# Gate products in halves around the update product of a triangular inverse, and five of ten conditioning quarters summed on GpSimd

## The reference, cut to what matters

```python
c_act = jax.nn.silu(c)
for layer in range(DEPTH):
    ada = c_act @ ada_w[layer] + ada_b[layer]             # 1024 x 6144 weights
    sh1, sc1, gt1, sh2, sc2, gt2 = jnp.split(ada, 6, axis=-1)
    h = modulate(rmsnorm(x, norm_mix_w[layer]), sh1, sc1)
    x = x + gt1[:, None, :] * token_mixer(h, ...)
    ...
# in token_mixer
t_mat = lax.linalg.triangular_solve(eye + lmat, eye, left_side=True, lower=True, unit_diagonal=True)
...
y = jax.nn.sigmoid(g_a) * (o_a @ w_a_out) + jax.nn.sigmoid(g_b) * (o_b @ w_b_out)
```

## Time and profile before

| | |
|---|---|
| median of 3 runs | 1731.92 us (1731.67 to 1734.11) |
| profiled execution | 1731.27 us, its span in the trace 1729.4 us |
| mean granted clock of PE | 0.989 |
| busy in the span: PE, DVE, ACT, POOL | 96%, 85%, 63%, 4% |
| the inverse of layer 0 in the trace | 134.14 to 199.09 us |
| the inverse of layer 1 | 609.24 to 674.18 us |
| the experts | from about 757 us to the end |

### The profile page before, as it was taken

How to read it: one execution, slowest core, us unless ns; L and a number is a source line. 1 busy time by engine, 2 the same in 40 slices (tenths; PEclk the granted TensorE clock), 3 DMA queues, 4 the chain that set the end, 5 groups by cost and what they waited for, 6 DMA issues and landing times.

```text
span 1729.4 us, 26895 instructions
## 1 busy us (share of the span) xinstructions
PE 1663.6 (96%) x10359; PEld 1447.7 (84%) x10362; DVE 1471.6 (85%) x1475; ACT 1084.4 (63%) x947; POOL 74.7 (4%) x132
## 2 busy tenths in 40 slices
PE   6998899999999988999999999999999999999997
PEld 6977799999998778987788888888888888888875
DVE  6979688887858696879998998999899989989998
ACT  4565345433445653566677777777777777777775
POOL 5010000000000100000000010000000000100000
PEclk8999999999999999999999999999999999999999
DMA  9746566888845365679999999999999999999994
GB/s 310 249 152 200 169 238 229 304 280 287 290 148 169 100 204 172 210 261 354 342 379 378 365 392 374 365 398 367 373 394 366 373 391 360 385 392 355 394 394 164
DMA packets 261449, 519.99 MB, mean 301 GB/s; under 512 B 12170, under 2 KB 75892, under 8 KB 261364
## 3 DMA queue, kind: packets, MB, share of 16 engines
q1 hardware_dynamic: 257988, 506.21, 82.2%
q0 software_dynamic: 3376, 12.58, 1.8%
HBM read 510.90 MB, written 7.86 MB: 300 GB/s over the span
## 4 chain that ended last, share of the span: by engine, by line
PE 80%; DVE 15%; issue 2%; ACT 2%; DMA 1%; POOL 0%; SPq 0%; DVEq 0%; ACTq 0%; POOLq 0%
PE bank L1156 17%; PE bank L1158 17%; PE bank L1157 17%; PE bank L1162 7%; PE bank L1163 7%; PE bank L1164 7%; DVE w_lo L1855 3%; DVE ada_acc L1873 3%; DVE w_lo L2048 2%; PE bank L1782 1%; DMA ring<-in_ada_w_dram 1%; ACT w_hi L1078 1%; PE bank L1312 0%; DVE hT_lo L1975 0%; DVE smax L2126 0%
## 5 line engine op out<-in xcount | busy, mean ns | idle before, releaser
L2048 DVE TENSOR_TENSOR w_lo<-ring,w_hi 128x2048 fp32r<-128x2048 f32 x336 | 764.3, 2289 | 84.0 <-ACT w_hi L1078 82.4
L1078 ACT CAST w_hi<-ring 128x2048 fp32r<-128x2048 f32 x336 | 643.3, 1915 | 125.0 <-PE bank L1158 113.5
L1156 PE MATMUL bank<-w_hi,xg_hi 128*128 128x512 f32 x896 | 353.0, 394 | 1.9 <-DVE w_lo L2048 1.0
L1158 PE MATMUL bank<-w_hi,xg_lo 128*128 128x512 f32 x896 | 349.2, 390 | 0.0
L1157 PE MATMUL bank<-w_lo,xg_hi 128*128 128x512 f32 x896 | 348.8, 389 | 0.0
L1162 PE MATMUL bank<-hT_hi,w_hi 128*128 128x256 f32 x1040 | 298.0, 287 | 8.1 <-DVE w_lo L1855 7.4
L1163 PE MATMUL bank<-hT_lo,w_hi 128*128 128x256 f32 x1040 | 292.2, 281 | 0.0
L1164 PE MATMUL bank<-hT_hi,w_lo 128*128 128x256 f32 x1040 | 292.0, 281 | 0.0
L1855 DVE TENSOR_TENSOR w_lo<-ring,w_hi 128x2048 fp32r<-128x2048 f32 x94 | 214.1, 2288 | 34.5 <-ACT w_hi L787 34.2
L787 ACT CAST w_hi<-ring 128x2048 fp32r<-128x2048 f32 x94 | 179.2, 1909 | 60.5 <-PE bank L1164 57.1
L1162 PEld LDWEIGHTS bank<-hT_hi,w_hi 128*128 128x128 f32 x1040 | 198.0, 190 | 12.4 <-issue 6.1
(11 more groups left out here) (451 smaller groups left out, 1903.5 us busy)
## 6 DMA issues: line engine op xcount, KB each, us to landing
ring<-in_moe_w_gate_dram SPq DMA_DIRECT2D x112, 1024.0 KB, 7.3
ring<-in_moe_w_up_dram SPq DMA_DIRECT2D x112, 1024.0 KB, 7.4
ring<-in_moe_w_down_dram SPq DMA_DIRECT2D x112, 1024.0 KB, 7.2
ring<-in_ada_w_dram SPq DMA_DIRECT2D x48, 1024.0 KB, 5.8
ring<-in_w_in_dram SPq DMA_DIRECT2D x38, 1024.0 KB, 5.8
ring<-in_ffn_w_gate_dram SPq DMA_DIRECT2D x14, 1024.0 KB, 5.7
ring<-in_ffn_w_up_dram SPq DMA_DIRECT2D x14, 1024.0 KB, 5.9
ring<-in_ffn_w_down_dram SPq DMA_DIRECT2D x14, 1024.0 KB, 5.4
```

What stands on the lines that cost most here:

```text
L1078: act.copy(w_hi[MOE_BUF[p % NS_MOE]][:], ring[:, p % RING, :]).then_inc(hi_ready, 1)
L1156: pe.matmul(o, xh, wh, start=start, stop=False)
L1158: return pe.matmul(o, xl, wh, start=False, stop=stop)
L2048: dve.tensor_tensor(w_lo[b][:], ring[:, p % RING, :], f32(w_hi[b][:]), ALU.subtract).then_inc(taken, 1)
```

## The change

It has four parts.

1. In the inverse, `two_blocks` of the gate unit becomes one block ahead of the update product and one behind it. The gate units' banks alternate for it (`GATE_BANK`), and each first half waits for an earlier sigmoid.
2. POOL sums five quarters: 5, 7 and 9 of layer 0, 4 and 10 of layer 1. For each unit it multiplies the four pieces in place in the ring, adds the upper half to the lower (128x1024) and the two pieces that are left (128x512) into `pool_acc`; for kh = 1 there is one more 128x512 addition. DVE still folds these quarters (`fold_from_pool`), each together with the next quarter of its own, except quarter 9. POOL begins with the transposed L of the inverse (`l0_ps`), and begins a further quarter when its last one is folded. SP waits for POOL's sum where it reloads such a slot.
3. Unit kh = 1 of quarter 9 moves from behind the first two mix units to between wb0 and wb1.
4. At the end of the dense SwiGLU, `ada_sum` moves one iteration ahead on PE, and DVE's `adac`, scale and router weights move from behind the loop into its last iteration.

```diff
+    GATE_BANK = (0, 0, 2, 0, 2, 0, 1)
...
+            if l == 0 and cc == 0:
+                ada_units(l, 1)
...
-                if l == 0 and (kh, cc) == (0, 1):
-                    ada_units(l, 1)
...
+    pool_q = ((5, 7, 9), (4, 10))
...
+            def sum_units(l):
+
+                for n, q in enumerate(pool_q[l]):
+                    if n == 0:
+                        pool.wait_ge(l0_ps, l + 1)
+                    else:
+                        pool.wait_ge(ada_folded, part_of[(l, pool_q[l][n - 1])] + 1)
+                    for kh in range(2):
...
+                        for kk in range(4):
+                            ins = pool.tensor_scalar(w[:, kk, :], w[:, kk, :], c_silu[:, 4 * kh + kk:4 * kh + kk + 1],
+                                                     None, ALU.mult)
+                        link(ins)
+                        link(pool.tensor_tensor(w[:, 0:2, :], w[:, 0:2, :], w[:, 2:4, :], ALU.add))
+                        if kh == 0:
+                            ins = pool.tensor_tensor(pool_acc, w[:, 0, :], w[:, 1, :], ALU.add)
+                        else:
+                            link(pool.tensor_tensor(w[:, 0, :], w[:, 0, :], w[:, 1, :], ALU.add))
+                            ins = pool.tensor_tensor(pool_acc, pool_acc, w[:, 0, :], ALU.add)
+                        ins.then_inc(pool_sum, 1)
...
-                    pe.wait_ge(gate_s, 8 * l + lev)
-                    two_blocks(("gate", l, lev), 0)
+                    pe.wait_ge(gate_s, 8 * l + max(lev - 1, 1))
+                    one_block(("gate", l, lev), GATE_BANK[lev], 0)
...
+                    one_block(("gate", l, lev), GATE_BANK[lev], 1)
-                pe.wait_ge(xx_s, 11 * (l + 1))
+                pe.wait_ge(xx_s, 12 * (l + 1))
...
-                        if i == 2 * FC - 1:
+                        if i == 2 * FC - 2:
                             ada_sum(8, 16, 3, 2 * P + 2)
...
+                if key in by_pool:
+                    return
...
+                    if ("ada", l, q - 1, 1) in by_pool and (l, q) != (0, NQ - 2):
+                        fold_from_pool(l, q - 1)
...
                 ahead(("wa", l, 1), 0)
+                if l == 0:
+                    fold_from_pool(0, 9)
...
                         ahead(("fg", i), 2)
+                        if i == 2 * FC - 1:
+                            ada_groups(1, 3, 2 * P + 2, (FFN_Q[:4], FFN_Q[4:]), NQA + 3)
+                            dve.wait_ge(ada_s, 4)
+                            norm_scale(2)
+                            fold_router()
```

More of the change, by code:

```diff
@@ L1 @@
+import itertools
 import math
@@ L117, in build_program @@
     u_of = {k: n for n, (k, _) in enumerate(units)}
+    pool_q = ((5, 7, 9), (4, 10))
+    by_pool = {("ada", l, q, kh) for l in range(L) for q in pool_q[l] for kh in range(2)}
+    took = list(itertools.accumulate(k not in by_pool for k, _ in units))
+    summed = list(itertools.accumulate(k in by_pool for k, _ in units))
+    T0 = took[-1]
     part_of = {}
@@ L292, in build_program @@
         XT_s = wk(9216, TB * H // 2, P)
+        pool_acc = wk(10240, 512)
         X = wk(8192, TB * H, P)
@@ L580, in load @@
                 if u >= RING:
-                    sp.wait_ge(taken, u - RING + 1)
                     old = units[u - RING][0]
+                    if old in by_pool:
+                        sp.wait_ge(pool_sum, summed[u - RING])
+                    else:
+                        sp.wait_ge(taken, took[u - RING])
                     if old[0] == "ada" and old[1] == 0 and old[2] < NQA - 1:
@@ L1878, in take, with fold, fold_from_pool @@
                 if kh == 1 and n >= NQA:
[L1879 to L1886 removed]
+                    if ("ada", l, q - 1, 1) in by_pool and (l, q) != (0, NQ - 2):
+                        fold_from_pool(l, q - 1)
+                    dve.wait_ge(taken, took[u])
+                    fold(part_of[(l, q)], acc)
+            def fold(m, acc):
+                if m:
+                    dve.wait_ge(ada_folded, m)
+                link(dve.transpose(ada_acc[:, 1, :], acc))
+                dve.tensor_reduce(ada_part[:, 16 * m:16 * m + 16],
+                                  ada_acc[:, 1, :].rearrange("p (b i) -> p b i", i=32), AX.X,
+                                  ALU.add).then_inc(ada_folded, 1)
+            def fold_from_pool(l, q):
+                dve.wait_ge(pool_sum, summed[u_of[("ada", l, q, 1)]])
+                fold(part_of[(l, q)], pool_acc)
             def take_upto(u):
```

42 lines of the change are left out of this document (19 added, 23 removed).

## The result

The changed kernel takes 1743.89 us (median of 3 runs, 1743.46 to 1747.07) against 1731.92 before: a ratio of 1.0072, 95% interval 1.0059 to 1.0086. The forecast was 1731.4 with a range of 1721 to 1738: the time is 12.5 us above the forecast and outside the range. The profiled execution took 1743.46 us at a span of 1741.7.

A forecast was written before the change was run, and what follows sets the result against it. DVE was taken to bound levels 1, 2, 3 and 5 of the inverse, PE the rest. Layer 0 +2.5, layer 1 -0.4 and SwiGLU's end -2.6 gave -0.5: 1730.8 profiled, 1731.4 as median, range 1721 to 1738.

The forecast's parts named there:

- 128x512 would take 0.58; I take 0.6: Price of POOL's one-input multiply, scaled from casts at 0.77 ns an element; its price may lie between 0.45 and 1.3.
- The dear rival: POOL's multiply takes 0.9 us or more, deciding from about 0.75; quarters 2.4 longer, total 1738; chance 0.22.
- the hold on level 4's scaling: Inverse level 4: DVE's path 7.9, about 9.0 with holds of 0.3 and 0.6; PE needs 9.1, so -0.8.
- Branches and fold, layer 0: Layer 0: branches +2.4 from POOL's holds, fold of quarter 9 +3.3, mix -1.2.
- The term of +3.3: Fold of quarter 9: DVE waits 2.4 for POOL and folds 1.4; PE's mix starts 3.3 later, bounds 0 and 6.
- Recurrence, layer 0: Recurrence of layer 0: DVE's path makes it 16.3 instead of 17.2, so -0.9.
- rival *clock: Waits of 3 us at the mix and 2.7 behind level 6 bring the low clock, 1 to 1.7 each: 1735; chance 0.08.
- Who stops whom: DVE instructions with two SBUF operands and POOL's wait for each other to the end; those with a PSUM operand are free.
- level 6: Level 6 to the recurrence's first product: 13.6 against 12.9, +0.7; a wait for ACT replaces one for DVE.
- Level 3: Inverse level 3: fold of quarter 5 adds 1.4, split held 0.5, scaling 0.6; +2.4, giving 12.5.
- The start of level 1: Start of the inverse's level 1: POOL's addition holds DVE, so U starts 0.9 later; bounds 0 and 1.3.
- The SwiGLU's end: End of the dense SwiGLU: the fold moves into DVE's idle time, last squares end sooner; -2.6 (-2 to -3.2).

The follow-up runs named there:

- copy kernel: Changed kernel with POOL's 40 multiplies by a column replaced by copies; total not compared, mixers 7.4 and 0.3 us longer than in the kernel before.
- POOL at one column: Changed kernel with POOL's multiplies and additions cut to one column of each tile; total not compared, mixers gain 2.5 and 1.1 us against the kernel before.
- late-fold kernel: Changed kernel with DVE's fold of quarter 9 moved ahead of the last mix unit's split: 1741.69 us, 1.0046 of the kernel before.
- the token copies first: Changed kernel with ACT's four token copies ahead of the sigmoid of gate unit 6: 1737.61 us, 1.0029 of the kernel before.
- the halves with the token copies first: Changed kernel without POOL's quarters, unit 9.1 back at the mix, ACT's token copies ahead of gate unit 6's sigmoid: 1724.28 us, 0.9948 of the kernel before.

## Why the prediction was wrong

**The mis-sized term: POOL's multiply.** The step that failed is "For one input ... 128x512 would take 0.58; I take 0.6". The casts were the wrong nearest row: the lone price is 1.56 us, above even the upper bound of 1.3 from the two-input rows. The prices for two inputs held (1.2 and 2.2 put in; 1.26 alone, 2.35 to 2.4 in after). The dear rival had the mechanism, from 0.75 us on, but its 0.9 us gave 1738; at the same 6.6 us for each 0.3, the upper bound of 1.3 that the prediction itself named would give an estimated 1747, and the range ended at 1738. The copy kernel shows what hung on it: 8.6 us. The Trainium skill, GPSIMD Engine Reference, section Engine selection, calls one-input forms "roughly line-rate". The copy, 610 ns, is 1.4 times the 0.43 us estimated from that, and the multiply by a column or a constant, 1564 and 1487 ns, 3.6 and 3.5 times: the measurement decides, and the page does not hold for this form.

**The second mis-sized term: the hold on level 4's scaling.** The sum had DVE's path in level 4 "with holds of 0.3 and 0.6 about 9.0", and the level at 9.1. It took 10.97 and 10.98 us in after, and 11.38 and 11.37 in the copy kernel, where POOL had the price of the sum: 2 us in either layer. DVE's split, scaling and update in layer 0 of after, POOL's addition beside them, and the stretch of level 4 in layer 1:

```profile
171.53 2.29 DVE L1894 TENSOR_TENSOR w_lo<-ring,w_hi 128x2048 fp32r<-128x2048 f32 x1 [2.62 <-ACT w_hi L824]
173.74 3.41 DVE L2262 TENSOR_TENSOR work<-work 128x1024 f32<-128x1024 f32 x1
177.08 0.74 DVE L2269 TENSOR_TENSOR work<-work,bank 128x256 f32<-128x256 f32 x2
...
172.24 3.83 POOL L745 TENSOR_TENSOR ring<-ring 128x1024 f32<-128x1024 f32 x1
...
652.80:663.78 10.98, 9.70 (x116) 9.17 (x116) 7.05 (x6) 4.26 (x4) 10.82 (x6) 0.80 1.04 352
```

POOL's 128x1024 addition waits for the split and then holds the scaling for its own length: 3.41 us where 1.22 was the earlier trace rows, 2.2 instead of the 0.6 put in. The rest is the cast, which ACT ends 4.6 us after the level's start instead of 3.75, since U and the turns ahead of it ran at the low clock (U 1.13 us, 0.69 before). The low clock does no more than this to the level: at 0.74 and 0.80 in the two layers it has the same length. Only where the scaling is not held does PE's clock decide: with POOL at one column the level is 10.03 us at 0.73 and 9.21 at 0.81, with PE busy throughout.

**Branches and fold, layer 0.** Forecast +2.4, +3.3, -1.2; measured 2.9, 8.2 and, in the stretch behind, 1.4. The first was right. POOL was done at 244.0 instead of 235.7, DVE asked at 235.8 instead of 233.3, and the wait was 8.23 instead of 2.4. The term of +3.3 had bounds of 0 and 6, and 8.2 lies outside them. The late-fold kernel shows that even without the wait 4.8 of the 8.2 stay: 3.5 as PE's longer wait for held DVE work, 1.3 as low clock (0.91). In the copy kernel the wait was 2.55 and the stretch to the mix 3.0 longer than before: the term was right at the price put in. In the mix PE ran at 0.88.

**Recurrence, layer 0.** Forecast -0.9, measured +0.2. The wait for ACT ahead of it was priced and the clock behind it was not: PE is busy 15.99 us at 0.90, and with the token copies first, without the wait, 14.32 at 1.00, so that the stretch takes 15.8 us instead of 17.4. Layer 1 had the same wait of 2.73 and a clock of 1.00 behind it. The rival *clock* (0.08) named waits at the mix and behind level 6 with 1 to 1.7 us each; this is one of them, and the mix the other.

**What held.** Who stops whom: multiply-adds, splits and scalings are held, instructions with an operand in PSUM are not (1562 ns beside them, 1564 alone). The Trainium skill (SBUF — State Buffer, section Who interferes with whom) states that only the port pair which DVE and POOL share causes contention, and as an exclusive lock; the held rows above agree with it, 3.41 us for the scaling beside POOL's addition among them. Level 1 (-2.35 for -2.5), level 5 (-1.84 for -1.8), level 6 (+0.59 for +0.7) with the first product of the recurrence waiting for ACT, and layer 1's recurrence (+1.0 for +0.7). Level 3 was 13.3 for 12.5, and not for the reasons given: its split and scaling took 2.28 and 1.22 us and were not held. POOL began quarter 7 only at 164.2, after 5.57 us without work until unit 7.0 had landed in the slot that it had freed at 158.6. What it added to the fold's 1.4 is 1.8 us of holds on the multiply-adds by the end of quarter 5. The start of level 1 lost nothing where 0.9 was put in. The SwiGLU's end gained 3.3, a little over the bound of 3.2: from the first product of the dense SwiGLU to the start of layer 1's level 1 it is 341.6 us before and 338.3 after, 338.2 and 338.6 in the two kernels without POOL, 341.9 where the move is undone. Kernels with the old end lie between 341.6 and 343.3, those with the new one between 338.2 and 339.5. PE's idle time there:

```profile
519.99 0.48 PE L1264 MATMUL bank<-f_sq,ones 128*128 128x256 f32 x1 [1.14 <-ACT f_sq L879]
```

It was 3.13 and is 1.14; about 1 was named.

**What stays open.** The stretches are read from one profile of each kernel, and the clock behind a wait is not the same from one execution to the next: single stretches differ by 1.6 us and more by it (last section). What decides it is not shown, and the share of the low clock in the 12 us was not taken apart from the waits that go with it.

## What to carry to other kernels

Moving work to POOL is not free for the engine that it relieves: in these traces DVE's work with two SBUF operands and POOL's multiplies, copies and additions take turns, so POOL's time is DVE's too wherever they meet, and the price of the exact form must be measured on the idle engine before it is trusted. A long POOL instruction can hold a short DVE one for its whole length, so a hold is bounded by that length and not by an average. Look first for the relieved engine's own idle gaps: here 0.87 us between a level's last update and the next U took in most of a fold, which gave 7 us on the kernel before and 12 on the halves with the token copies first. All of it together, with the SwiGLU's end, is 20 us below the kernel before, where the halves with 141 us of POOL's work lost 12. And where a step is split in halves around a product, follow what the second half now stands ahead of.
